# A two-layer decoder step on one core: seven moves in the order of the work, and three of eight tiles of each layer's embedding projection computed between the mixer's norm and the MLP

## The reference

```python
def run(x, p, sample):
    for i in range(2):
        h = rms_norm(x, norm_g[i, 0])
        if i == 0:    # conformer: GLU(h @ pw1), causal depthwise conv of 31 taps, layer norm, silu, @ pw2
            m, st_new = conv_module(h, st, ...)
        else:         # native sparse attention, prompt or sample
            m, r_c, r_s, r_w = nsa_prompt(h, ...) or nsa_sample(h, cache_cmp, cache_sel, cache_win, page_table, ...)
        x = x + rms_norm(m, norm_g[i, 1])
        f = relu(rms_norm(x, norm_g[i, 2]) @ w_ff1[i]) ** 2 @ w_ff2[i]
        x = x + rms_norm(f, norm_g[i, 3])
        gate = sigmoid(x @ w_ple_gate[i] + b_ple_gate[i])
        x = x + gate * (p[i] @ w_ple[i])       # the embedding projection: p[i] is 256 wide
```

## Time and profile before

| what | value |
|---|---|
| median of 3 runs | 1828.74 us (1827.53 to 1831.94) |
| the profiled execution | 1830.59 us, span 1828.8 us |
| mean granted clock of PE over the span | 0.967 |
| PE busy | 1721.0 us, 94% of the span |
| DVE, ACT, POOL busy | 41%, 34%, 33% |
| DMA | 180.07 MB, 98 GB/s over the span |

### The profile page before, as it was taken

One profiled execution on the slowest core, in us unless ns is written; L12 is line 12 of the kernel. 1 busy time (PEld: TensorE's weight loads), 2 busy tenths in 40 slices (PEclk: granted clock), 3 DMA queues, 4 the chain that ended last, 5 costly groups with the idle time before them and its releaser, 6 DMA issues.

```text
span 1828.8 us, 31143 instructions
## 1 busy us (share of the span) xinstructions
PE 1721.0 (94%) x13303; PEld 1587.1 (87%) x13303; DVE 758.4 (41%) x1153; ACT 618.1 (34%) x972; POOL 600.8 (33%) x286
## 2 busy tenths in 40 slices
PE   6999999899999999998998878999889999999988
PEld 5997879799999999897998545556879999999978
DVE  4999933530212122455054656776161020312242
ACT  4211035432322223244222445775342231313232
POOL 4541322133334333232333003555313334343322
PEclk9998999899999999998999998999989999999999
DMA  7239603123332222121227771001212222222211
GB/s 246 93 106 143 214 19 120 70 92 139 116 115 71 92 71 91 47 93 70 82 76 248 253 247 48 2 1 48 82 47 93 70 93 75 87 92 70 93 54 68
DMA packets 61274, 180.07 MB, mean 98 GB/s; under 512 B 22850, under 2 KB 23762, under 8 KB 47250
## 3 DMA queue, kind: packets, MB, share of 16 engines
q1 hardware_dynamic: 60466, 177.18, 29.5%
q10 hardware_dynamic: 128, 0.88, 0.3%
q0 software_dynamic: 544, 0.03, 0.0%
HBM read 167.02 MB, written 16.45 MB: 100 GB/s over the span
## 4 chain that ended last, share of the span: by engine, by line
PE 84%; DVE 4%; SPq 3%; DMA 3%; ACT 2%; issue 2%; POOL 1%; ACTq 0%; DVEq 0%
PE ps L669 22%; PE ps L671 22%; PE ps L670 22%; PE ps L782 5%; PE ps L1036 2%; PE ps L1064 2%; PE ps L715 2%; PE ps L1047 2%; POOL w_lo L592 1%; DMA attn_t<-in_win 1%; SPq L536 1%; SPq L509 1%; DMA big<-v_kept 1%; PE ps L893 1%; ACT w_hi L1105 1%
## 5 line engine op out<-in xcount | busy, mean ns | idle before, releaser
L592 POOL TENSOR_TENSOR w_lo<-w_raw,w_hi 128x2048 fp32r<-128x2048 f32 x98 | 452.8, 4621 | 890.9 <-ACT w_hi L1105 890.9
L669 PE MATMUL ps<-ha,w_hi 128*128 128x288 f32 x1920 | 576.4, 300 | 29.9 <-DVE hb L1466 13.0
L670 PE MATMUL ps<-hb,w_hi 128*128 128x288 f32 x1920 | 572.5, 298 | 0.0
L671 PE MATMUL ps<-ha,w_lo 128*128 128x288 f32 x1920 | 572.1, 298 | 0.0
L669 PEld LDWEIGHTS ps<-ha,w_hi 128*128 128x128 f32 x1920 | 366.9, 191 | 37.5 <-issue 25.9
L670 PEld LDWEIGHTS ps<-hb,w_hi 128*128 128x128 f32 x1920 | 367.2, 191 | 0.0
L671 PEld LDWEIGHTS ps<-ha,w_lo 128*128 128x128 f32 x1920 | 367.1, 191 | 0.0
L669 PE MATMUL ps<-hid_hi,w_hi 128*128 128x288 f32 x1024 | 301.8, 295 | 0.0
L671 PE MATMUL ps<-hid_hi,w_lo 128*128 128x288 f32 x1024 | 301.7, 295 | 0.0
L670 PE MATMUL ps<-hid_lo,w_hi 128*128 128x288 f32 x1024 | 301.7, 295 | 0.0
L1105 ACT ACTIVATE w_hi<-w_raw 128x2048 fp32r<-128x2048 f32 x98 | 186.9, 1907 | 174.0 <-PE ps L671 165.1
(11 more groups left out here) (242 smaller groups left out, 1986.5 us busy)
## 6 DMA issues: line engine op xcount, KB each, us to landing
w_raw<-in_w SPq DMA_DIRECT2D x98, 1024.0 KB, 4.8
ring<-in_sel_pages SPq DMA_DIRECT2D x64, 256.0 KB, 4.0
ring<-in_cmp_pages SPq DMA_DIRECT2D x40, 256.0 KB, 4.5
attn_t<-in_win SPq DMA_DIRECT2D x16, 512.0 KB, 6.7
cmp_hb<-in_cmp_pages SPq DMA_DIRECT2D x16, 256.0 KB, 4.2
x<-in_x SPq DMA_DIRECT2D x4, 576.0 KB, 5.8
out_y<-x SPq DMA_DIRECT2D x8, 288.0 KB, 2.1
big<-in_cmp_pages SPq DMA_DIRECT2D x8, 256.0 KB, 4.1
```

The lines of the kernel that those rows point to most:

```text
L592: nc.gpsimd.tensor_tensor(w_lo[j % 2][:, :], w_raw[:, k, :], w_hi[j % 2][:, :].bitcast(F32), ALU.subtract).then_inc(w_ready, 1)
L669: nc.tensor.matmul(to, wh, chunk(hi, k, a * HT, HT), start=k == 0, stop=False)
L670: nc.tensor.matmul(to, wh, chunk(lo, k, a * HT, HT), start=False, stop=False)
L671: return nc.tensor.matmul(to, wl, chunk(hi, k, a * HT, HT), start=False, stop=k == C - 1)
```

## The change

Seven moves, and an eighth part:

1. The stores of `conv_p` and `conv_s` stand on SP's queue behind page 3 and no longer behind page 1.
2. The units go in another order (the last three sequences' keys, then their values); the layer norm's mean stands behind unit 11, `stats(1)` behind unit 14, `spread(1)` in the middle of unit 15, and the last `compress_out` in the middle of pw2's first two tiles. DVE centres all eight chunks before it adds their squares; ACT's silus, splits and evictions move with that.
3. ACT splits the MLP's third weight block (`up` + 2) right after the norm's std and not later in the MLP.
4. `post_norm` of the MLP gives each lo part of the gate's input right behind its chunk, ACT each hi part between evictions of the embedding's tiles; `stats` of that norm moves behind the second tile of `ple`, `spread` behind the third.
5. `kv_pairs` is laid out in two parts, keys when v_tok's first block is split, values behind the `w1` load; PE waits for each alone, and for the compressed keys alone before the scores.
6. `win_k` of a sequence is loaded before its pages, one round earlier; the stores of k_rot and v_tok move to its third.
7. The prompt attention has 48 steps: for the query blocks 0 and 1 both branches are one step, with one mask, one maximum and one move for both.
8. Three tiles of each layer's embedding projection are computed before the MLP, one before `stats`, one before `spread`, one behind it, from their own copy of the weight's first 384 columns (`w_ahead`, an extra DMA `first_columns`); they go through the slots of the MLP's first tiles, and ACT copies each to `emb_ahead`.

```diff
+AHEAD = 3
+STAGES = ([("pw1", 16, "A" * 16), ("pw2", C, "A" * C)] + mlp_stages(0) + [("ple0", C - AHEAD, "A" * (C - AHEAD)), ("gate0", C, "A" * C),
           ("q", C, "A" * C), ("kv_cmp", 4, "A" * 4), ("k_rot", 4, "A" * 4), ("gates", 1, "A"), ("v_tok", 2 * TT, "A" * 2 * TT),
           ("gates_t", 1, "A"), ("out", C, "A" * C)] + mlp_stages(1)
-          + [("ple1", C, "A" * C), ("gate1", C, "A" * C)])
+          + [("ple1", C - AHEAD, "A" * (C - AHEAD)), ("gate1", C, "A" * C)])
...
         BLOCKS += [("w1", 0), ("sel_pages", 0), ("win_k", 0), ("win_v", 0), ("win_k", 1), ("sel_pages", 1), ("win_v", 1),
-                   ("sel_pages", 2)]
+                   ("sel_pages", 2), ("win_k", 2)]
         for _b in range(2, NB):
-            BLOCKS += [("win_k", _b)] + [("sel_pages", _b + 1)] * (_b + 1 < NB) + [("win_v", _b)]
+            BLOCKS += [(_s2, _b + 1) for _s2 in ("win_k", "sel_pages") if _b + 1 < NB] + [("win_v", _b)]
...
-PAIRS = [(c, r, n) for c in range(C) for n in range(PT) for r in range(2)]
-PER_C = 2 * PT
+PAIRS = [(c, rs, n) for c in range(C) for rs, n in [((0, 1), 0), ((0, 1), 1), ((0,), 2), ((1,), 2), ((0,), 3), ((1,), 3)]]
...
+            def first_columns(layer):
...
+            def pair_rows(v):
...
+                sp.wait_ge(w_ready, W_OF["v_tok"] + v + 1)
+                for e in range(2):
+                    for later in range(2):
+                        sp.dma_start(kv_pairs[64 * later:64 * later + 64, 1 - v, e:e + 3:2, 0:SEQ - later],
+                                     kv_cmp[64 * e:64 * e + 64, 2 * v:2 * v + 2, later:SEQ]).then_inc(pairs_in[v], 16)
...
                 if (src, row) == ("w1", 0):
-                    sp.wait_ge(w_ready, W_OF["out"])
                     sp.wait_ge(act_freed, FREED[FIRST["kv_cmp"] + 3][1])
-                    for e in range(2):
-                        for later in range(2):
-                            sp.dma_start(kv_pairs[64 * later:64 * later + 64, :, e:e + 3:2, 0:SEQ - later].rearrange(
-                                             "p v g t -> p (v g) t"),
-                                         kv_cmp[64 * e:64 * e + 64, :, later:SEQ]).then_inc(pairs_in, 16)
+                    pair_rows(0)
...
-                if (src, row) == ("cmp_pages", 1):
+                if (src, row) == ("cmp_pages", 3):
                     sp.wait_ge(glu_done, 2 * C)
                     sp.dma_start(out["conv_p"], conv_in[:, :, SEQ:EXT_P]).then_inc(conv_stored, 16)
                     for m in range(C):
                         sp.dma_start(out["conv_s"][:, m], sample_rows(m)[:, :, DT:]).then_inc(conv_stored, 16)
...
+                    sp.wait_ge(sample_conv, C)
+                    first_columns(0)
...
+                    first_columns(1)
                 if (src, row) == ("w1", 0):
+                    pair_rows(1)
                     sp.wait_ge(rot_done, 12)
                     sp.wait_ge(cmp_stored, 16 * 2)
-                    sp.dma_start(k_cmp_s, k_kept.rearrange("p b (g c) -> p b g c", g=2)).then_inc(cmp_in, 16)
-                    sp.dma_start(v_cmp_s, v_kept).then_inc(cmp_in, 16)
+                    sp.dma_start(k_cmp_s, k_kept.rearrange("p b (g c) -> p b g c", g=2)).then_inc(cmp_in[0], 16)
+                    sp.dma_start(v_cmp_s, v_kept).then_inc(cmp_in[1], 16)
+                if (src, row) == ("win_k", 2):
                     sp.dma_start(out["k_rot"], k_rot[:, :, :]).then_inc(kept_out, 16)
-                if (src, row) == ("sel_pages", 2):
                     sp.wait_ge(act_freed, FREED[FIRST["v_tok"] + 2 * TT - 1][1])
                     sp.dma_start(out["v_tok"], v_tok[:, 0:PT, :]).then_inc(kept_out, 16)
                     sp.dma_start(out["v_tok_s"], v_tok[0:NS, PT, :]).then_inc(kept_out, 16)
...
-                if m == EARLY[-1]:
-                    split_weights(C, C + 1)
                 prompt_convolved(pool, m)
...
                     nc.gpsimd.tensor_tensor(sq_sum[:, :], so_far, y[:, m, :], ALU.add).then_inc(y_added, 1)
-            split_weights(C + 1, W_OF["out"])
+            split_weights(C, W_OF["out"])
...
+                    if beside is not None and k == C // 2:
...
+                    if m == 2 and beside is not None:
+                        pe.wait_ge(w2_out, 2 * NB)
...
-                for m in range(C):
-                    if m == 1:
+                for m in range(AHEAD, C):
+                    if m == AHEAD + 1:
+                        stats(norm)
+                    elif m == AHEAD + 2:
...
+            def ahead(layer, m):
+                t = FIRST[f"up{layer}0"] + m % 2
+                if m < 2:
+                    slot_free(t)
+                else:
+                    pe.wait_ge(ahead_out, AHEAD * layer + m - 1)
+                if m == 0:
+                    pe.wait_ge(ple_loaded, 16 * (layer + 1))
+                    pe.wait_ge(w_ahead_in, 16 * (layer + 1))
+                for a in range(2):
+                    for k in range(2):
+                        last = nc.tensor.matmul(slot(t)[:, a, :], w_ahead[:, k, m * P:(m + 1) * P],
+                                                ple_in[:, k, a * HT:(a + 1) * HT], start=k == 0, stop=k == 1)
+                last.then_inc(ahead_mm, 1)
+            def into_mlp(layer, norm):
+                ahead(layer, 0)
+                stats(norm)
+                ahead(layer, 1)
+                spread(norm)
+                ahead(layer, 2)
+                pe.wait_ge(ahead_out, AHEAD * (layer + 1))
...
                 for half in range(2):
+                    if half == 1 and u == 2 * NB - 1:
+                        compress_out(u - 1)
+                        spread(1)
...
-            for u in range(2 * NB - 2):
+            def mean():
+                pe.wait_ge(conv_done, C)
...
+            for u in range(2 * NB):
                 if u < 2:
...
-                if u >= 1:
+                if 1 <= u < 2 * NB - 1:
...
-            last.then_inc(mean_ready, 1)
-            for u in (2 * NB - 2, 2 * NB - 1):
-                compress(u)
-                compress_out(u - 1)
-            compress_out(2 * NB - 1)
-            stats(1)
-            spread(1)
-            dense("pw2")
-            stats(2)
-            spread(2)
+                if u == 2 * NB - 5:
+                    mean()
+                if u == 2 * NB - 2:
+                    stats(1)
+            pe.wait_ge(hid_ready, 2 * NB - 1)
+            pe.wait_ge(w2_out, 2 * NB - 1)
+            dense("pw2", beside=lambda: compress_out(2 * NB - 1))
+            into_mlp(0, 2)
             mlp(0)
-            stats(4)
             ple(0, 4)
             dense("gate0")
...
+            pe.wait_ge(cmp_in[0], 16)
...
             block_there(B_OF["w1", 0])
-            pe.wait_ge(pairs_in, 16 * 4)
             for v in range(2):
+                pe.wait_ge(pairs_in[v], 16 * 4)
...
+                    for e in range(2):
+                        part = slice(64 * e, 64 * e + 64)
...
+                                                k_rot[part, 2 * r + c // 4, 0:(n + 1) * P], start=True, stop=True)
+                last.then_inc(p_mm, 1)
...
                     p_out(i - 4)
             dense("out")
-            stats(6)
-            spread(6)
+            into_mlp(1, 6)
...
@@ -1143,6 +1208,7 @@
                                          scale=pcol("norm_g", C * (2 + 4 * layer) + k)).then_inc(hi_ready, 1)
                     square(n, k, x[:, k, :])
                 std(n)
+                split_weight(W_OF[f"up{layer}0"] + 2)
...
@@ -1176,8 +1242,12 @@
                         nc.scalar.activation(halves(mix[:, m, :]), p, ACT.Identity, bias=pcol(bias, m)).then_inc(act_freed, 1)
                     act.wait_ge(act_freed, FREED[FIRST[stage] + m][1])
                     square(n, m, mix[:, m, :])
-                split_weight(W_OF["up00" if stage == "pw2" else "up10"] + 1)
+                layer = 0 if stage == "pw2" else 1
+                split_weight(W_OF[f"up{layer}0"] + 1)
                 std(n)
+                for m in range(AHEAD):
+                    act.wait_ge(ahead_mm, AHEAD * layer + m + 1)
+                    nc.scalar.activation(halves(emb_ahead[:, m, :]), slot(FIRST[f"up{layer}0"] + m % 2), ACT.Copy).then_inc(ahead_out, 1)
             def mlp(layer, norm):
                 for n in range(Q4):
...
-            def x_hi(name, update):
-                for k in range(C):
...
-            def ple(layer):
...
+                def out_of(m):
+                    p = tile(f"ple{layer}", m)
+                    nc.scalar.activation(halves(emb[:, C - count + m, :]), p, ACT.Copy).then_inc(act_freed, 1)
+                out_of(0)
+                out_of(1)
                 for m in range(C):
-                    p = tile(f"ple{layer}", m)
-                    nc.scalar.activation(halves(emb[:, m, :]), p, ACT.Copy).then_inc(act_freed, 1)
+                    hi_part(f"x{layer}", m, x[:, m, :], (x_ready, C * update + m + 1))
+                    if m + 2 < count:
```

(61 more changed lines are left out.)

152 lines of the change are left out of this document (81 added, 71 removed).

## The result

The changed kernel takes 1778.55 us (median of 4 runs, 1773.53 to 1784.14), the kernel before 1830.34 in the same comparison: ratio 0.9717, 95% interval 0.9681 to 0.9753. Forecast were 1778 and a range of 1764 to 1796.

A forecast was written before the change was run, and what follows sets the result against it. PE was taken as the bound over most of the span, with time to win where it idles or runs at a low clock. Terms −12.5 −10.4 −8 −14 −6 = −50.9 from 1830.6, less 1.85 as median, gave 1778 us; range 1764 to 1796.

The forecast's parts named there:

- Compression and pw2: From the compression to pw2, moves 1 and 2: pw2 starts earlier, −12.5 us, bounds 8 and 15.
- 6.8 in it for the stores: Before unit 4: with the stores behind page 3, 3.82 us of idle time and 2.97 us after it go.
- The later split of pw2's first block costs nothing: At pw2's start: POOL's 4.54 us for a block end before 265, so no cost.
- Norm and MLP: Norm and MLP start, moves 3 and 8: −5.2 us a layer (4.4 early split, 0.8 clock), −10.4 us in all.
- MLP's end to the gate: Between MLP and gate, moves 4 and 8: −8 us over two layers, with about 4.1 us waiting for w_lo left.
- Attention prelude: Before the sample attention, move 5: keys laid out one block earlier, scores at about 991, −5 us.
- Sample rounds: Sample attention's eight rounds, move 6: the wait for a window goes, 88.2 us falls by 8.6.
- SP's cycle sets the pace: Sample attention: with win_k a round ahead, each of eight rounds takes 9.95 us, five of them reading page numbers.
- a sample stretch still over 85 us: Sample attention: a sign named beforehand that would show the prediction wrong.
- Rival 1: Sample attention: rounds stay at the transfers' pace, only 5 us come from before them, 1787 us; chance 0.13.
- Prompt attention: Prompt attention, move 7: sixteen steps fewer save fixed time per group, −6 us, bounds −12 and +5.
- 16 x 2 x 0.22: Prompt attention: sixteen steps fewer save 0.22 us each in transposes and values products, 7 us at most.

The follow-up runs named there:

- The late split: Changed kernel, but ACT splits the MLP's third weight block where it did before the change: median 1787.74 us.
- The two runs that shorten SP's cycle: Changed kernel with page numbers read for the first sequence only, 1775.38 us; changed kernel with pw2's later split, gate's split halved, POOL issuing half the pages, 1764.49 us.
- the halves: Changed kernel with pw2's split one unit later and the gate's second weight block split in two halves of 128 columns: 1768.29 us.

## Why the prediction was right, and where it was not

- **Compression and pw2.** The mechanism holds, and both profiles lie beside the term, −15.1 and −10.6 for −12.5. Of the 6.8 in it for the stores 4.4 are shown. What was missed is in the sentence "The later split of pw2's first block costs nothing": it ends in time for pw2, but can run into DVE's end of the convolution, as it did in three of eight profiles. The cover of 1 us that the prediction named was the narrow place.
- **Norm and MLP.** As forecast, −10.9 for −10.4. The late split gives 8.7 of it back, and the tiles ahead are not needed for it: without them nearly all of it stays (0.5 us less in layer 1). So the 0.8 us of clock a layer that the prediction counted for a TensorE that doesn't stand idle before the MLP is not shown to come from the tiles; where the rest beyond the split comes from is open.
- **MLP's end to the gate.** −8.2 for −8, with the wait of 3.74 us for the 4.1 forecast. The prediction did not draw the last step from its own numbers: if the gate waits for w_lo whatever TensorE does before, the moved tiles are worth nothing there. The first gate tiles end at 26.1 us after the MLP and w_lo comes at 29.9, so of 5.9 us moved away 3.74 became waiting, and smaller waits and the lower clock behind it (1.3 to 2.6 us, forecast 1.6) took more than the rest. The gain of the stage is move 4's: without the tiles ahead it is larger, 72.0 to 66.3.
- **Attention prelude.** Mechanism right, 1.4 us more: the scores don't wait at all.
- **Sample rounds: the failed step** is "SP's cycle sets the pace", with 9.95 us for every round. Rounds start, in the changed kernel, 4.8, 8.6, 10.8, 10.3, 14.1, 9.9 and 10.4 us after each other, and the last takes 15.9; before 4.8, 9.0, 11.4, 11.5, 12.8, 13.1, 9.8 and 15.8. Only five follow the loads; one of them holds an idle time of TensorE that was there before the change, too, and the wait for windows was exchanged for one for pages. The five paced rounds took 58.6 us together before and 55.5 after. By the prediction's own sign, "a sample stretch still over 85 us", the term was wrong in nine of the ten profiles with these rounds and loads. PE's waits in this stretch before,

```profile
PE ps L940 <- DMA attn_t<-in_win: 4.6, 3, 2.7
PE ps L1021 <- issue: 3.4, 1, 3.4
```

and after (us in total, times, longest):

```profile
PE ps L1005 <- DMA ring<-in_sel_pages: 4.7, 3, 2.2
PE ps L1087 <- issue: 4.2, 1, 4.2
```

 Rival 1 was nearer here. The two runs that shorten SP's cycle show that the cycle is a part of the pace, 81.2 and 79.9 us for 84.8 to 88.1.
- **Prompt attention: the mis-sized term.** "16 x 2 x 0.22" counts transposes and value products. The scores are a third group with a fixed time: two of 0.49 us became one of 0.71, which is 0.27. 16 x (0.27 + 0.22 + 0.22) = 11.4; that is an estimate on the high side, since a group's length overlaps the next group's start by some 0.07 us in these rows. The rest of the 13 goes with fewer small waits: the idle time of the stretch is 7.8 us before and 5.5 after. DVE and ACT did not become the bound, and the clock stayed at 1.00 in the columns behind the first.

That the sum met the median to 1 us is luck: a miss of +6 and one of −7, and the tiles ahead, which were to be part of the gain, gave nothing.

## What to carry to other kernels

Before work is moved out of a stage, ask what ends that stage when the work is gone: here it was a weight split on two other engines, and the moved tiles paid only when that was cut into halves. TensorE's wait of 3.74 us cost 5.0 to 6.3 us here, since its clock was lower behind it, and the tiles that fill it in the run without tiles ahead are free. A step moved to a place where "it has time" can block a small instruction of another engine, as POOL's subtraction did with DVE's: look for what runs there in the same microsecond, and at a margin of 1 us expect the result to differ from run to run.

## What was not expected of the hardware

- An instruction of DVE of 0.25 us takes 2.96 when POOL's subtraction has begun before it, and one of 0.76 takes 4.60.
- Waiting 3.74 us costs TensorE 1.3 to 2.6 us more in the six gate tiles that follow: 39.7 to 41.1 us for them in the profiles with the wait, and 38.4 with a wait of 0.75 us (the halves, layer 1).
- In 13 of the 14 profiles TensorE stands idle for 3.4 to 4.7 us at one instruction between the starts of the fifth and the sixth sample round, without a semaphore that explains it; in the other one, with the old order of the windows, it waits 3.62 us for a window right there. In each of the 13 a packet of 16 KB, on a DMA queue that the profile calls "instruction", moves within the idle time, and TensorE goes on 1.2 to 1.5 us after its end. Late loading of instructions is therefore likely, but no run here tried it.
